# The triangular inverse of a chunked RWKV-7 scan: full 128x128 products against compact 32x32 diagonal blocks

## Chip, cores and metric

One core of a Trainium2 chip runs the whole program. The metric is the device time of one execution in microseconds (us). TensorE multiplies, VectorE and ScalarE work elementwise, GpSimd and SyncE here only issue DMAs. All operands of this part are fp32; the profile shows an fp32 product as two records of weight load and matmul.

## What is computed

Two transformer blocks follow each other on 256 tokens of width 2048; the second has 16 meta tokens in front. Its mixer has an RWKV-7 half and a "fox" attention half. The recurrence of the first, per head of 64 channels (16 heads, 272 tokens), is

```python
def step(S, inp):
    r_t, w_t, k_t, v_t, a_t, b_t = inp
    sa = jnp.einsum('bhvk,bhk->bhv', S, a_t)
    S = (S * w_t[:, :, None, :] + sa[..., None] * b_t[:, :, None, :]
         + v_t[..., None] * k_t[:, :, None, :])
    return S, jnp.einsum('bhvk,bhk->bhv', S, r_t)
_, y = lax.scan(step, jnp.zeros((B, H, N, N), F32), xs)
```

Beside it stand the projections `proj = xn @ w_in`, of which the fox columns (24 tiles of 128) and the gate columns (32 tiles) are computed during the scan.

## The kernel before

**The scan in chunks.** `rwkv_pe`, `rwkv_act` and `rwkv_dve` (L1698, L1973, L2077) hold one stream per engine. A loop over j takes two heads at a time, eight steps in all. The tokens come in a chunk of 16 (meta) and two of 128. Within a chunk the recurrence is solved with the inverse of I - N, N being the strictly upper triangular Gram matrix of b and a, decay included. Index q = 2h + c names head h and chunk c, so a step has four matrices of 128x128 and, for the meta tokens, one of 64x64 that holds two of 16x16 (head h at rows and columns 32h).

**Order of a step on TensorE.** Sums of decays (L1740), the bonus (L1745), transposes to token order (L1752, L1756), the Gram products (L1771, L1773: 64-row halves; L1778: meta, into bank 4), then the inversion, then "x0", "u0", "s0" for the meta chunk (L1843 to L1855), and for each of the chunks "x", "u", "y", state (L1864 to L1891).

**The inversion.** `gm` holds the masked Gram matrices; `upper8` cuts out the 8x8 diagonal blocks, whose inverse comes from the products p2, p4, r (N squared, its square, and the product of the sums). Then blocks are joined to 16, 32, 64, 128: with the inverse R so far and the joining part of N (masks `join16` to `join128`), one product P and one product D per join give the new R. VectorE transposes R between them within 32x32 blocks (`T_`). `product` (L1788) runs over the two matrices of a head, `of_head` (L1783) adds the meta matrix; all products are 128x128x128 up to the join of 64:

```python
for m in (16, 32, 64):
    for h in range(2):
        pe.wait_ge(*rd.after(((f"rt{m // 2}" if m > 16 else "rt", h), j)))
        product(h, 0, 2, 1, m == 16).then_inc(*rp.did(((f"p{m}", h), j)))
        if m > 16 and h == 0:
            side(1)
    for h in range(2):
        pe.wait_ge(*ra.after(((f"p{m}", h), j)))
        last = product(h, 0, 3, 0, m == 16)
```

The last join works on half the columns (L1830, L1837). ScalarE copies the banks to `inv_s` (`step`, L2028 to L2036; L2056 for the last), VectorE masks, adds the identity, transposes (L2137 to L2211). `gram_mask(n, h)` (L2135) masks half of the Gram matrices of a head, 128x512 in one operation: `gram_mask(0, .)` the products of b, which the inversion needs, `gram_mask(1, .)` those of k, which are needed first at L1864.

**Side work.** `side(n)` lets n slots of the projections pass. On TensorE a slot is one call of `side_mm` (L529): six matmuls, 128x128 weights against 272 or 256 columns, lines L538, L540, L542. On ScalarE (`side_hi`, L520) and VectorE (`side_lo`, L525) one operation of 128x512 comes with every second slot; every eighth slot VectorE also takes a finished tile (L1640, L2662). ScalarE's operation waits until TensorE has used the same quarter of the buffer two tiles before. The `side` calls in the three streams are written out by hand; a step has 31 slots on each engine, whichever kernel. They all have to be done; what the scan doesn't take is done behind it.

**Waits.** Each engine counts its own steps in one semaphore (`Order`: `rd` VectorE, `ra` ScalarE, `rp` TensorE), and the order of the steps is written out in `INV_DVE`, `INV_ACT` and `PE_INV`. An engine's stream is executed in order.

## Time and profile before

| | |
|---|---|
| median of 3 executions | 2949.26 us (2948.57 to 2949.82) |
| the profiled execution | 2952.27 us |
| its span, first to last instruction | 2950.2 us |
| mean granted clock of TensorE | 0.997 |
| first Gram product of the first to that of the eighth scan step | 1407.59 to 1775.74 us of the span: 368.15, 52.6 a step |

The page gives for each engine the union of its instructions' times. Rows of a view of lines read: line, engine, operation, out<-in, shapes, count, then busy us, mean ns of one, and idle time ahead with what ended it. Matmuls overlap, so a record is longer than the distance to the next one. PE is TensorE, PEld its weight loads, DVE VectorE, ACT ScalarE.

### The profile page before, as it was taken

Reading aid. Unit: us, or ns where it says so; the run is one execution under the profiler, and the core shown is the slowest. Engines: PE = TensorE matmul, PEld = TensorE weight load, DVE = VectorE, ACT = ScalarE, POOL = GpSimd, SP = SyncE. Lnnn points to the kernel's source line nnn. Section 1 sums busy time; section 2 is a strip of 40 time slices with the busy share of each in tenths; the row PEclk is TensorE's granted clock in tenths of the full one; section 3 lists DMA queues with packets and bytes.
Section 4 is the critical chain, followed back from the end, with each engine's and each line's share of the span. In section 5 each row is a group of like instructions: output and inputs, shape, how many; then the busy total and the mean of one; then the engine's idle time right before and its main releaser. Section 6 shows DMA issues by size and latency. Waiting matters only on the chain.

```text
span 2950.2 us, 51319 instructions
## 1 busy us (share of the span) xinstructions
PE 2917.3 (99%) x21485; PEld 2697.7 (91%) x21485; DVE 1786.5 (61%) x2680; ACT 1251.0 (42%) x1860; POOL 53.2 (2%) x102
## 2 busy tenths in 40 slices
PE   9999999999999999999999999999999999999999
PEld 8999998888889999999898888889998888889999
DVE  5567757566656445755666666666666655665444
ACT  5355444333333344544333443455444333333433
POOL 1000000000000000000000000000000000000000
PEclk9999999999999999999999999999999999999999
DMA  7665445555555555455333335444555555555553
GB/s 240 196 174 166 158 157 174 186 189 182 194 185 185 185 185 186 143 178 149 83 97 87 83 89 139 119 135 156 188 187 180 184 189 187 187 178 197 185 184 132
DMA packets 370314, 484.96 MB, mean 164 GB/s; under 512 B 12359, under 2 KB 181654, under 8 KB 370150
## 3 DMA queue, kind: packets, MB, share of 16 engines
q1 hardware_dynamic: 362752, 471.55, 50.5%
q0 software_dynamic: 4112, 7.88, 0.9%
q10 hardware_dynamic: 3302, 3.39, 0.4%
q8 instruction: 113, 1.85, 0.3%
q14 instruction: 35, 0.29, 0.0%
HBM read 475.76 MB, written 7.01 MB: 164 GB/s over the span
## 4 chain that ended last, share of the span: by engine, by line
PE 91%; DVE 6%; issue 1%; ACT 1%; DMA 0%; DVEq 0%; SPq 0%; ACTq 0%
PE psum L333 19%; PE psum L339 12%; PE psum L338 12%; PE psum L337 12%; PE psum L335 10%; PE psum L538 5%; PE psum L542 5%; PE psum L540 5%; PE psum L1789 3%; DVE w_lo L323 2%; DVE arena L711 1%; PE psum L1771 0%; DVE arena L699 0%; PE psum L2584 0%; DVE act L786 0%
## 5 line engine op out<-in xcount | busy, mean ns | idle before, releaser
L323 DVE TENSOR_TENSOR w_lo<-w_raw,w_hi 128x1024 fp32r<-128x1024 f32 x728 | 858.9, 1221 | 798.2 <-ACT w_hi L314 798.2
L314 ACT ACTIVATE w_hi<-w_raw 128x1024 fp32r<-128x1024 f32 x728 | 731.3, 1052 | 1163.3 <-PE psum L335 592.1
L333 PE MATMUL psum<-act,w_hi 128*128 128x512 f32 x2816 | 990.0, 394 | 8.6 <-issue 4.5
L337 PE MATMUL psum<-act,w_hi 128*128 128x256 f32 (+2 forms) x3024 | 855.3, 283 | 6.7 <-issue 4.5
L339 PE MATMUL psum<-act,w_lo 128*128 128x256 f32 (+2 forms) x3024 | 856.3, 283 | 0.0
L338 PE MATMUL psum<-act,w_hi 128*128 128x256 f32 (+2 forms) x3024 | 856.3, 283 | 0.0
L335 PE MATMUL psum<-act,w_lo 128*128 128x256 f32 x2816 | 790.9, 281 | 0.0
L333 PEld LDWEIGHTS psum<-act,w_hi 128*128 128x128 f32 x2816 | 529.9, 188 | 136.4 <-DVE w_lo L323 11.1
L337 PEld LDWEIGHTS psum<-act,w_hi 128*128 128x128 f32 (+1 forms) x3024 | 572.4, 189 | 10.9 <-issue 8.2
L339 PEld LDWEIGHTS psum<-act,w_lo 128*128 128x128 f32 (+1 forms) x3024 | 572.9, 189 | 0.0
L338 PEld LDWEIGHTS psum<-act,w_hi 128*128 128x128 f32 (+1 forms) x3024 | 569.2, 188 | 0.1
L335 PEld LDWEIGHTS psum<-act,w_lo 128*128 128x128 f32 x2816 | 530.5, 188 | 0.1
L538 PE MATMUL psum<-act,w_hi 128*128 128x256 f32 (+1 forms) x1280 | 390.6, 305 | 0.0
L542 PE MATMUL psum<-act,w_lo 128*128 128x256 f32 (+1 forms) x1280 | 362.4, 283 | 0.0
L540 PE MATMUL psum<-act,w_hi 128*128 128x256 f32 (+1 forms) x1280 | 362.0, 283 | 0.0
L520 ACT ACTIVATE w_hi<-w_raw 128x512 fp32r<-128x512 f32 x320 | 195.6, 628 | 235.4 <-PE psum L542 222.7
L538 PEld LDWEIGHTS psum<-act,w_hi 128*128 128x128 f32 x1280 | 242.1, 189 | 20.4 <-issue 14.6
L525 DVE TENSOR_TENSOR w_lo<-w_raw,w_hi 128x512 fp32r<-128x512 f32 x320 | 211.8, 681 | 78.7 <-ACT w_hi L520 78.3
L540 PEld LDWEIGHTS psum<-act,w_hi 128*128 128x128 f32 x1280 | 242.2, 189 | 1.1
L542 PEld LDWEIGHTS psum<-act,w_lo 128*128 128x128 f32 x1280 | 241.6, 189 | 0.0
L699 DVE TENSOR_REDUCE arena<-psum 128x256 f32<-128x512 f32 x176 | 112.9, 683 | 15.0 <-PE psum L335 14.0
L1789 PE MATMUL psum<-arena 128*128 128x128 f32 (+1 forms) x800 | 113.3, 280 | 2.0 <-DVE arena L2179 0.9
(381 smaller groups left out, 1732.3 us busy)
## 6 DMA issues: line engine op xcount, KB each, us to landing
w_raw<-w_in SPq DMA_DIRECT2D x128, 1024.0 KB, 5.7
w_raw<-w_down SPq DMA_DIRECT2D x88, 1024.0 KB, 5.1
w_raw<-w_gate_up SPq DMA_DIRECT2D x88, 1024.0 KB, 5.0
w_raw<-w_gate SPq DMA_DIRECT2D x44, 1024.0 KB, 5.1
w_raw<-w_up SPq DMA_DIRECT2D x44, 1024.0 KB, 5.1
w_raw<-w_out SPq DMA_DIRECT2D x16, 1024.0 KB, 5.1
w_raw<-w_o SPq DMA_DIRECT2D x16, 1024.0 KB, 5.1
w_raw<-w_branch_a SPq DMA_DIRECT2D x8, 1024.0 KB, 5.1
```

Source lines behind the costliest of these rows:

```text
L314: nc.scalar.activation(w_hi[:, s % 2, 2 * h:2 * h + 2, 0:wd], w_raw[:, s % RAW, 2 * h:2 * h + 2, 0:wd], ACT.Copy).then_inc(hi_ready, 1)
L323: nc.vector.tensor_tensor(w_lo[:, s % 2, 2 * h:2 * h + 2, 0:wd], w_raw[:, s % RAW, 2 * h:2 * h + 2, 0:wd], w_hi[:, s % 2, 2 * h:2 * h + 2, ...
L333: pe.matmul(dst.rearrange("p (h n) -> p h n", h=2), w1, both_parts, start=first, stop=False, skip_group_check=True)
L335: return pe.matmul(dst[:, 0:n], w0, act_hi[:, k, tok], start=False, stop=last, skip_group_check=True)
L337: pe.matmul(dst, w1, act_hi[:, k, tok], start=first, stop=False, skip_group_check=True)
L338: pe.matmul(dst, w1, act_lo[:, k, tok], start=False, stop=False, skip_group_check=True)
L339: return pe.matmul(dst, w0, act_hi[:, k, tok], start=False, stop=last, skip_group_check=True)
L525: nc.vector.tensor_tensor(side_view(w_lo, u % 2, 4 * n, 4), side_view(w_raw, u % RAW, 4 * n, 4), side_view(w_hi, u % 2, 4 * n, 4).bitcast( ...
L538: pe.matmul(dst, hi[:, k], act_hi[:, k, tok], start=k == 0, stop=False, skip_group_check=True)
L540: pe.matmul(dst, hi[:, k], act_lo[:, k, tok], start=False, stop=False, skip_group_check=True)
L542: mm = pe.matmul(dst, lo[:, k], act_hi[:, k, tok], start=False, stop=k == KT - 1, skip_group_check=True)
L1789: return of_head(h, meta, lambda q, m: pe.matmul(ps(bank, q, m), sl(l, q, m), sl(r_, q, m), start=True, stop=True))
```

## The change

The diagonal 32x32 blocks of all matrices are kept compactly: a tile of 128 partitions x 5 x 32 holds, for block b at partitions 32b to 32b + 31 and slot q, the diagonal block b of matrix q; slot 4 holds the meta blocks of the two heads. Up to the join of 32 eight products (p2, r1t, p4, s8, v16, s16, v32, s32) work on these, each block by a 32x32 tile of the array. The factors are the transposed ones, which VectorE makes out of the banks (`turned`). The raw diagonal blocks come from products of their own ("blocks"), ahead of the Gram products. The joins of 64 and 128 are made of products of 32x32 and 64x64 tiles. The table keeps its size (`room`). The diff, cut to its core. Tables and places:

```diff
+    parts["upper8"] = (i < j) & (i // 8 == j // 8)
+    joins = []
+    for m in (16, 32):
+        join = (i // m == j // m) & (i % m < m // 2) & (j % m >= m // 2)
+        joins.append(join * 1.0 - ((i // (m // 2) == j // (m // 2)) & (i < j)))
+    parts["joins"] = np.concatenate(joins, axis=1)
+    parts["ident_blocks"] = i == j
+    parts["room"] = np.zeros((P, 640))
...
+        raw = place(6, BLOCK)
+        (n8, n8t, i8t, p2, p2t, ip2, ip4, r1t, s8) = (place(5, BLOCK) for _ in range(9))
+        nm = place(2, 5, BLOCK)
+        nm16, nm32 = nm[:, 0], nm[:, 1]
+        s8t, v16, s16, s16t, v32, s32t = n8t, p2, p2t, ip2, ip4, n8
+        inv_t, inv64 = place(4, P), place(4, 2 * BLOCK)
+        v64, v128 = place(4, BLOCK), place(4, 2 * BLOCK)
```

TensorE: "blocks" (head 0 from partitions 0 to 63, head 1 from 64 to 127) and the meta products; then the Gram products as before, and the inversion with its waits (`dve(n)` and `act(n)` wait for that step of VectorE or ScalarE):

```diff
+                for b in range(4):
+                    for c in range(2):
+                        t = slice(META + c * P + BLOCK * b, META + c * P + BLOCK * b + BLOCK)
+                        for h, r in enumerate(hs):
+                            pe.matmul(psum[rows32(b), 5 - h, cols32(c)], bh[r, t], ar[r, 0, t],
+                                      start=True, stop=True)
+                for n, src in enumerate((bh, kh)):
+                    for h, r in enumerate(hs):
+                        mm = pe.matmul(psum[mh[h], 5 - h, 64 + n * META:64 + (n + 1) * META], src[r, 0:META],
+                                       ar[r, 0, 0:META], start=True, stop=True)
+                mm.then_inc(*rp.did(("blocks", j)))
...
+                def product(bank, l, r_, step, nq=5):
+                    for q in range(nq):
+                        for b in range(4 if q < 4 else 2):
+                            mm = pe.matmul(psum[rows32(b), bank, cols32(q)], l[rows32(b), q], r_[rows32(b), q],
+                                           start=True, stop=True)
+                    mm.then_inc(*rp.did((step, j)))
...
+                dve("n8t")
+                product(4, n8t, n8, "p2")
+                side(1)
+                dve("ip2")
+                product(5, ip2, i8t, "r1t")
+                act("p2")
+                product(4, p2t, p2, "p4")
+                side(1)
+                dve("ip4")
+                act("r1t")
+                product(4, r1t, ip4, "s8")
+                side(1)
+                dve("s8t")
+                product(5, nm16, s8t, "v16")
+                side(1)
+                act("v16")
+                product(4, v16, s8, "s16")
+                side(1)
+                dve("s16t")
+                product(5, nm32, s16t, "v32", 4)
+                side(1)
+                act("v32")
+                product(4, v32, s16, "s32", 4)
+                side(1)
+                dve("s32t")
+                for q in range(4):
+                    for b in (0, 2):
+                        mm = pe.matmul(psum[rows32(b + 1), 0, cols32(q)], gm[rows32(b), q, cols32(b + 1)],
+                                       s32t[rows32(b), q], start=True, stop=True)
+                mm.then_inc(*rp.did(("v64", j)))
+                side(1)
+                dve("v64")
+                act("s32")
+                for q in range(4):
+                    mm = pe.matmul(psum[rows32(1), 0, cols32(q)], inv_t[rows32(1), q, cols32(1)],
+                                   v64[rows32(1), q], start=True, stop=True)
+                mm.then_inc(*rp.did(("x64t", j)))
+                for q in range(4):
+                    for b in (0, 2):
+                        mm = pe.matmul(psum[rows32(b), 1, cols32(q)], v64[rows32(b + 1), q],
+                                       inv_t[rows32(b + 1), q, cols32(b + 1)], start=True, stop=True)
+                mm.then_inc(*rp.did(("x64", j)))
+                side(1)
+                low, high = slice(0, 64), slice(64, P)
+                dve("x64t")
+                act("x64")
+                for h in heads:
+                    for c in range(2):
+                        q = 2 * h + c
+                        mm = pe.matmul(psum[high, h, 64 * c:64 * c + 64], gm[low, q, high], inv64[low, q],
                                        start=True, stop=True)
+                    mm.then_inc(*rp.did((("v128", h), j)))
+                side(1)
+                for h in heads:
+                    if h:
+                        act("v128")
+                    else:
+                        dve("v128")
+                    for c in range(2):
+                        q = 2 * h + c
+                        mm = pe.matmul(psum[low, 4 + h, 64 * c:64 * c + 64], v128[high, q], inv_t[high, q, high],
                                        start=True, stop=True)
+                    mm.then_inc(*rp.did((("x128", h), j)))
+                side(1)
+                dve("gm0")
...
+                for h in range(2):
+                    mm = pe.matmul(psum[rows32(h), 1, 0:RHD], s16[rows32(h), 4], xs[rows32(h), 0],
+                                   start=True, stop=True)
...
+                    act("x128")
```

ScalarE; v16, s16 (after s16t), v32, s32 (after s32t, four copies by rows), x64 (two), v128 and x128 of head 1 follow with `side(1)` between them:

```diff
-                side(6)
+                side(4)
+                def copy(dst, src):
+                    return s.activation(dst, src, ACT.Copy)
+                def evac(step, of, dst, bank, nq=5):
+                    s.wait_ge(*of)
+                    copy(dst, blocks_of(bank, nq)).then_inc(*ra.did((step, j)))
+                s.wait_ge(*PEA("blocks"))
+                copy(raw[:, 0:2], blocks_of(5, 2))
+                copy(raw[mh[0], 4:6, 0:META], psum[mh[0], 5, 64:64 + 2 * META].rearrange("p (n t) -> p n t", n=2)) \
+                    .then_inc(*ra.did(("raw0", j)))
+                side(1)
+                evac("p2", rd.after(("p2t", j)), p2, 4)
+                side(1)
+                evac("r1t", PEA("r1t"), r1t, 5)
+                side(1)
+                evac("s8", rd.after(("s8t", j)), s8, 4)
```

VectorE:

```diff
-            v.memset(inv_m_all, 0.0)
+            v.memset(raw, 0.0)
+            v.memset(inv_t, 0.0)
+            v.memset(inv64, 0.0)
...
+                v.wait_ge(*PEA("blocks"))
+                v.wait_ge(*rd.after("gm_zero"))
+                v.tensor_copy(raw[:, 2:4], blocks_of(4, 2))
+                v.tensor_copy(raw[mh[1], 4:6, 0:META],
+                              psum[mh[1], 4, 64:64 + 2 * META].rearrange("p (n t) -> p n t", n=2)) \
+                    .then_inc(*D_("raw1"))
+                v.wait_ge(*A_("raw1"))
+                v.wait_ge(*ra.after(("raw0", j)))
+                TT(n8, raw[:, 0:5], table_of("upper8"), ALU.mult).then_inc(*D_("n8"))
+                v.wait_ge(*A_("n8"))
+                v.transpose(n8t, n8).then_inc(*D_("n8t"))
+                v.wait_ge(*A_("n8t"))
+                TT(i8t, n8t, table_of("ident_blocks"), ALU.add).then_inc(*D_("i8t"))
+                v.wait_ge(*PEA("p2"))
+                TT(ip2, blocks_of(4, 5), table_of("ident_blocks"), ALU.add).then_inc(*D_("ip2"))
+                v.transpose(p2t, blocks_of(4, 5)).then_inc(*D_("p2t"))
+                TT(nm, raw[:, 0:5].unsqueeze(1).broadcast_to([P, 2, 5, BLOCK]),
+                   T["joins"].rearrange("p (n t) -> p n t", n=2).unsqueeze(2).broadcast_to([P, 2, 5, BLOCK]),
+                   ALU.mult).then_inc(*D_("nm"))
+                side(1)
+                v.wait_ge(*A_("nm"))
+                TT(nm, nm, T["ident_blocks"].unsqueeze(1).unsqueeze(1).broadcast_to([P, 2, 5, BLOCK]), ALU.add) \
+                    .then_inc(*D_("nm_diag"))
+                v.wait_ge(*PEA("p4"))
+                TT(ip4, blocks_of(4, 5), table_of("ident_blocks"), ALU.add).then_inc(*D_("ip4"))
+                v.wait_ge(*PEA("gram"))
+                gram_mask(0, 0)
+                side(1)
+                gram_mask(0, 1).then_inc(*D_("gram"))
+                def turned(step, of, dst, nq=5):
+                    v.wait_ge(*PEA(of))
+                    v.transpose(dst, blocks_of(4, nq)).then_inc(*D_(step))
+                turned("s8t", "s8", s8t)
+                side(1)
+                gram_mask(1, 0)
+                turned("s16t", "s16", s16t)
                 side(2)
+                turned("s32t", "s32", s32t[:, 0:4], 4)
+                v.wait_ge(*A_("s32t"))
+                for b in range(2):
+                    v.tensor_copy(inv64[rows32(b), :, cols32(b)], s32t[rows32(b), 0:4])
+                for h in range(2):
+                    ins = TT(gm0[mh[h], 0, mh[h]], raw[mh[h], 5, 0:META], mask[mh[h], mh[h]], ALU.mult)
+                ins.then_inc(*D_("gm0"))
```

Behind it come, each after its wait: the copy v64, `side(1)`, x64t, `gram_mask(1, 1)`, `side(1)`, v128 of head 0, `side(1)`, x128 of head 0, `side(2)`.

## Rows read from the trace of the kernel before

**Rows 1.** The page, part 1 and the chain of part 4 by engine.

```profile
PE 2917.3 (99%) x21485; PEld 2697.7 (91%) x21485; DVE 1786.5 (61%) x2680; ACT 1251.0 (42%) x1860; POOL 53.2 (2%) x102
...
PE 91%; DVE 6%; issue 1%; ACT 1%; DMA 0%; DVEq 0%; SPq 0%; ACTq 0%
```

**Rows 2.** Windows p2 to x0, eight steps: us, busy us per engine, clock, DMA.

```profile
1464.10:1488.17 24.07, 23.59 (x182) 21.95 (x183) 17.11 (x49) 10.68 (x30) 0.55 (x1) 1.00 0.21 56
...
1728.25:1751.59 23.34, 23.08 (x182) 21.39 (x183) 17.00 (x49) 10.98 (x31) 0.00 (x0) 1.00 0.17 46
...
sum 190.24, PE 187.30 PEld 174.24 DVE 136.60 ACT 86.97 POOL 4.39; mean PE 23.41 PEld 21.78 DVE 17.07 ACT 10.87 POOL 0.55
```

**Rows 3.** TensorE's timeline, step 2: start us, us, what, count.

```profile
1464.78 0.29 PE L540 MATMUL psum<-act,w_hi 128*128 128x272 f32 x1
...
1466.17 2.37 PE L1789 MATMUL psum<-arena 128*128 128x128 f32 x14
...
1478.97 1.05 PE L1789 MATMUL psum<-arena 128*128 128x128 f32 x8
1479.78 0.37 PE L538 MATMUL psum<-act,w_hi 128*128 128x272 f32 x1
```

**Rows 4.** TensorE's timeline, step 3; the last row is cut at 1515.33.

```profile
1511.22 0.51 PE L1756 MATMUL psum<-tab,arena 64*16 64x64 f32 x12
...
1513.16 0.29 PE L542 MATMUL psum<-act,w_lo 128*128 128x272 f32 x1
1513.38 0.43 PE L1771 MATMUL psum<-arena 64*64 64x256 f32 x2
1513.39 0.43 PE L1773 MATMUL psum<-arena 64*64 64x256 f32 x2
1513.64 0.38 PE L1771 MATMUL psum<-arena 64*64 64x256 f32 x2
...
1513.86 0.38 PE L1771 MATMUL psum<-arena 64*64 64x256 f32 x2
...
1515.26 0.27 PE L1778 MATMUL psum<-arena 64*16 64x16 f32 x8
1515.46 0.39 PE L538 MATMUL psum<-act,w_hi 128*128 128x272 f32 x1
1515.69 0.29 PE L540 MATMUL psum<-act,w_hi 128*128 128x272 f32 x1
...
1517.26 0.71 PE L1789 MATMUL psum<-arena 128*128 128x128 f32 x4
...
1515.26 0.23 PE L1778 MATMUL psum<-arena 64*16 64x16 f32 x5
```

**Rows 5.** Lines by form of step 3: count, busy us, mean ns of one.

```profile
L1756 PE MATMUL psum<-tab,arena 64*16 64x64 f32 x12 | 0.5, 218 | 0.0
...
L1778 PE MATMUL psum<-arena 64*16 64x16 f32 x8 | 0.3, 176 | 0.0
```

**Rows 6.** VectorE's timeline, step 3, as rows 3.

```profile
1515.58 0.69 DVE L2137 TENSOR_TENSOR arena<-psum,tab 128x512 f32<-128x512 f32 x1 [1.29 <-PE psum L1778]
...
1516.76 0.45 DVE L2174 STREAM_TRANSPOSE arena<-arena 128x256 f32<-128x256 f32 x1
```

**Rows 7.** Lines by form of VectorE, then ScalarE, seven steps: as rows 5.

```profile
L525 DVE TENSOR_TENSOR w_lo<-w_raw,w_hi 128x512 fp32r<-128x512 f32 x108 | 72.7, 675 | 7.6 <-ACT w_hi L520 7.6
L2137 DVE TENSOR_TENSOR arena<-psum,tab 128x512 f32<-128x512 f32 x28 | 18.7, 668 | 14.3 <-PE psum L1778 14.3
...
L2191 DVE TENSOR_TENSOR arena<-psum,tab 128x256 f32<-128x256 f32 x14 | 5.3, 416 | 0.2
...
L1640 DVE TENSOR_TENSOR arena<-psum,rstd 128x272 f32<-128x272 f32 x11 | 4.7, 424 | 0.1
...
L2211 DVE COPY arena<-psum 64x128 f32<-64x128 f32 x14 | 4.0, 283 | 12.1 <-PE psum L1837 12.1
...
L2032 ACT ACTIVATE arena<-psum 128x256 f32<-128x256 f32 x126 | 48.3, 383 | 69.6 <-PE psum L1789 68.9
```

More of the change, by code:

```diff
@@ L1589, in transformer_pair_kernel @@
         heads = range(2)
-        INV_DVE = [("gram", 0), ("n8", 0), ("nt8", 0), ("gram", 1), "gram0", ("n8", 1), ("nt8", 1),
-                   ("p2t", 0), ("ip2", 0), ("int8", 0), ("int8", 1), ("p2t", 1), ("ip2", 1),
-                   ("less", 0), ("less", 1), ("nm16", 0), ("nm16", 1), ("ip4", 0), ("ip4", 1)]
-        INV_ACT = ["p2", "r1t", "r"]
-        for m in (16, 32, 64):
-            INV_ACT += [f"p{m}", f"r{m}"]
-            INV_DVE += [(n, h) for n in ["rt" if m == 16 else f"rt{m // 2}", f"nm{2 * m}"][:1 + (m < 64)]
-                        for h in heads]
-        INV_DVE += [(n, h) for n in ("rt64", "r128") for h in heads]
-        INV_ACT = [(n, h) for n in INV_ACT + ["p128"] for h in heads]
+        INV_DVE = ["raw1", "n8", "n8t", "i8t", "ip2", "p2t", "nm", "nm_diag", "ip4", "gram", "s8t", "s16t",
+                   "s32t", "gm0", "v64", "x64t", "v128", "x128"]
+        INV_ACT = ["raw0", "p2", "r1t", "s8", "v16", "s16", "v32", "s32", "x64", "v128", "x128"]
         for j in range(8):
@@ L1614, in transformer_pair_kernel @@
         rw_pe_steps = ["kksum"]
-        PE_INV = ["p2", "p4", "r"]
-        for m in (16, 32, 64, 128):
-            PE_INV += [f"p{m}", f"d{m}"]
-        PE_INV = [(n, h) for n in PE_INV for h in heads]
+        PE_INV = ["p2", "r1t", "p4", "s8", "v16", "s16", "v32", "s32", "v64", "x64t", "x64",
+                  ("v128", 0), ("v128", 1), ("x128", 0), ("x128", 1)]
         rw_pe_steps += [("logits", 0), ("kkspread", 0)]
         for j in range(8):
-            rw_pe_steps += [(n, j) for n in ["sums", "bonus", "toks", "gram"] + PE_INV
+            rw_pe_steps += [(n, j) for n in ["sums", "bonus", "toks", "blocks", "gram"] + PE_INV
                             + ["x0", "u0", "s0", "x1", "u1", "y1s1", "x2", "u2", "y2"]]
@@ L2206, in rwkv_dve @@
[L2206 to L2214 removed]
+                TT = v.tensor_tensor
```

225 lines of the change are left out of this document (53 added, 172 removed).

## The prediction

> **What bounds the kernel now.** I read the page first: TensorE is busy in 99% of a span of 2950.2 us and makes 91% of the chain that ended last; VectorE is at 61%, ScalarE at 42% [rows 1]. So time is saved only where TensorE has less to do, or waits less. Next, the stretches: in each of the eight scan steps the inversion, from its first product to the product "x0", takes 23.34 us (step 7), 24.07 (step 2) and the like, in all eight 190.24, at a granted clock of 1.00 throughout, with TensorE busy for 187.30 of them [rows 2]. Within such a stretch two kinds of work share TensorE: the inversion's own products, and 11 slots of side work (six matmuls of the fox and gate projections each), which must be done somewhere in any case. Side matmuls start 0.126 us apart (11 from 1464.78 to 1466.17), so a slot is 0.76 us and 11 are 8.3 us. What is left, 23.8 - 8.3 = 15.5 us per step, is what the change can touch. A full 128x128 fp32 product is two records, 0.101 us apart (8 in 0.81 us) [rows 3].
>
> **What tiles cost.** The trace shows small tiles at work already. In the Gram products (L1771, L1773) four records of 256 columns on four 64x64 quarters start within 0.02 us of each other, and the next four 0.26 later, then 0.22: four tiles run side by side. L1756 (64 rows x 16 columns, 64 columns moving) alternates between two halves of the rows and writes one bank: 12 records are through in 0.51 us, one lasts 0.218, so starts are (0.51 - 0.22)/11 = 0.027 us apart, half of what a record of 64 columns needs alone (half of the 0.106 of 128 columns). So two run at a time, in one bank. L1778 (16 columns) has 8 records in 0.27 us, one lasting 0.176: 0.013 apart, 0.025 a pair; five have started 0.07 us after the first [rows 4, 5]. Changing between full and tiled work costs: side to tile, 0.22 between starts (1513.16 to 1513.38) for 0.13; tile to side, 0.11 from L1778's last start (0.27 - 0.18 = 0.09 after its first at 1515.26) to the side matmul at 1515.46, and 0.23 instead of 0.13 to the one after it [rows 4]. Together some 0.30 us for each tiled product between two side slots.
>
> The Trainium skill ("TensorEngine Tiling (Array Packing)", Gotcha 1) says that different row tiles cannot access one PSUM bank at the same time. The new products put all four diagonal tiles into one bank, so by that rule they would run one by one; the pairs of L1756 speak against it. That case is a rival below.
>
> **Removed per step:** 50 products in ten rounds, eight half-wide ones, one of u0, i.e. the 15.5 us, waits among them.
>
> **Added per step, on TensorE.** 32 columns are a quarter of 128, so 0.027 us a record; I take 0.03 us for a batch of four tiles (one record each), from the 0.025 of L1778's pairs and four starts at 0.007 each. A product over five blocks is 18 matmuls, 36 records, ten batches: 0.29 us.
> - p2, s8, v16, s16: 4 x (0.30 + 0.29) = 2.36
> - r1t and p4, back to back: 0.30 + 0.58 = 0.88
> - v32, s32 (four blocks): 2 x (0.30 + 0.24) = 1.08
> - v64 (two tiles, 16 records): 0.30 + 0.20 = 0.50
> - x64t (one tile, 8 records) and x64 (two, 16): 0.30 + 0.43 = 0.73
> - v128, x128 (one 64x64 tile each, 8 records of 64 columns at 0.053): 2 x (0.30 + 0.43) = 1.46
>
> Sum 7.0 us. Besides: "blocks", 16 more products ahead of the Gram ones, 32 records in pairs 0.43, one more change of tiling, 0.5; u0 by two tiles 0.2. The small Gram products are moved ahead, not added. The 11 side slots stay 11. The extra clearing on VectorE before the scan is some 570 elements a partition more: 0.6 us at most by the slope of its operations (0.283 for 128, 0.42 for 256 elements [rows 7]), beside side work, taken as nothing; if that cover fails it is 0.6 once.
>
> So without waits 15.5 - 7.0 - 0.5 - 0.2 = 7.8 us a step are saved.
>
> **Waits.** Each product now hands over to VectorE (or VectorE, then ScalarE) and TensorE covers with one side slot, 0.76 + 0.20 of the change back = 0.96 us. From a product's last start to VectorE's start it takes 0.22 us (L1778's last by 1515.36, L2137 at 1515.58), from the end of an operation to the product that waits for it 0.05 (1516.76 + 0.45 to 1517.26) [rows 4, 6]. An operation over 160 elements is 0.32 by the same slope, a copy by ScalarE 0.30 (0.383 for 256 [rows 7]). A hand-over with one operation is 0.22 + 0.32 + 0.05 = 0.6: covered. With a transpose and then ScalarE's copy it is 0.95, just covered, or covered by the next product too (p2t and p2 lie beside r1t). The transposes read the bank directly, so one copy less stands in the chain.
> The hand-over that isn't covered is s8 to v16. VectorE's queue is: ip4, Gram mask, side slot, Gram mask, then s8t. Each mask is 0.668, a side slot on the mean 0.39 (0.675 every second, a take of 0.43 every eighth) [rows 7]. From the start of ip4 that makes 0.32 + 0.67 + 0.39 + 0.67 + 0.32 + 0.05, less 0.25 for overlaps of successive operations: 2.2 us. TensorE in that time waits 0.37 for ip4, does s8 (0.50) and a slot (0.76): 1.6. Behind the wait stand v16 and everything after it. So 0.5 us a step, up to 1.1 where the slot holds both a difference and a take. ip4 itself stands behind nm, a side slot and the diagonal: late by 0 to 0.6. For ip4 and the joins (v64 behind inv64, gm0 and a side slot) I add 0.5: 1.0 in all. VectorE loses some 7 us of work per step (some 27 operations of 0.4 for 18 of 0.2 to 0.45), so it doesn't become the bound as a whole; nor does ScalarE. Blocks come 1.9 us before the Gram products end, so the first operations lie beside these and two slots: p2 doesn't wait.
>
> **The sum.** 7.8 - 1.0 = 6.8 us a step, 8 x 6.8 = 54 us. The profiled execution took 2952.3; 2898 would be left. It stands 3.0 over the median of the runs, 2949.3, so the forecast is 2895 us. After the scan nothing is touched: the same slots have been used.
>
> **Rivals.**
> (A) One tile at a time. 352 records of 32 columns at 0.027 are 9.5 us instead of the 3.3 in my sum: 6.2 more, against which the waits (1.0) are then hidden. 7.8 - 6.2 = 1.6 a step, 12 us: 2937. For it: no row has four 32x32 tiles, or more than 8 small records in a run. Against it: the pairs and fours of [rows 4]. Chance 0.12.
> The skill's page "TensorE: Matmul & The Clock Gate" ("Wait - 56ns, not 53.3ns?") has a floor of about 25 ns between starts however small the product is; by it the time would be about that of this case. L1778's 0.013 us goes below it.
> (B) Slower: supply of instructions. 184 small matmuls are 368 records with as many weight loads. The fastest longer run in the trace is the 40 records from 1513.38 to 1515.46: 0.052 us each [rows 4]; that more can be supplied for 36 in a row isn't shown, since the 8 of L1778 may have been waiting in the queue. At 0.052 they take 19.1 us instead of 4.1, 15 more: 7.2 lost a step, 58 us: 3007. It decides from (4.1 + 7.8)/368 = 0.032 us a record. Against it: those 40 were bound by their own columns, and nothing there waits for supply. Chance 0.07.
> (C) The waits take over: ten hand-overs each 0.3 us beyond the cover, 3 us a step instead of 1.0: 4.8 x 8 = 38, 2911. For it: the old rounds had the other head's product as cover too; VectorE's side operations stand ahead of most transposes. Against it: at most one hand-over works out as uncovered. Chance 0.28.
> The forecast's own case, 2884 to 2902, has 0.53.
>
> **Numbers.** Lower end: all 7.8 us and batches a little faster, 8.2 x 8: 2884. Upper end: (C) whole and (A) in part, 2930; outside stay most of (A) and (B), under 0.2. What a measurement here can tell from no change is 0.2%, 5.9 us. Faster by more: the forecast, (C) and nearly all of (A), 0.91; within: 0.03; slower: 0.06.
>
> **What would show it.** In the stretch from p2 to x0: some 16.3 us a step instead of 23.8, five-block products with 36 records in 0.3 us plus a record's 0.17, starts in fours 0.007 apart; the wait of v16 for s8t as the longest of TensorE in the scan, some 0.5 us. (A) would show starts 0.027 apart, (B) gaps with no releaser ("issue") within a product, (C) waits for VectorE or ScalarE at most products. The forecast is wrong if a five-block product takes over 0.6 us, or if TensorE's waits pass 1.5 us a step.

## The result and the profile after

| | before | changed |
|---|---|---|
| median of four runs, us | 2949.54 (2948.57 to 2949.84) | 2901.72 (2900.59 to 2912.38) |
| profiled execution / its span | 2952.3 / 2950.2 | 2902.6 / 2900.6 |
| records of TensorE | 21485 | 23517 |
| last "yc" product of the scan, from the span's start | 1816.27 | 1762.27 |
| from there to the products of the last gate slice | 39.00 | 42.88 |

The ratio of the changed kernel's time to the time before is 0.9845, 95% interval 0.9834 to 0.9857: faster by 1.6%. The median is 6.7 us above the forecast of 2895 and inside the range. Run once more the changed kernel gave 2899.16.

The page of the changed kernel, its engines, the chain by engine, and the queue that carries instructions, against [rows 1]:

```profile
PE 2862.3 (99%) x23517; PEld 2636.6 (91%) x23517; DVE 1734.1 (60%) x2522; ACT 1223.4 (42%) x1788; POOL 53.0 (2%) x102
...
q8 instruction: 129, 2.11, 0.3%
...
PE 91%; DVE 6%; issue 1%; ACT 1%; DMA 1%; DVEq 0%; SPq 0%; ACTq 0%
```

TensorE does 9% more records in 55 us less of busy time. It is as full as before, so what is read next is where it waits and what a tiled product costs.

The windows from p2 to x0, all eight steps (bounds, us, busy us of each engine, clock, DMA share and GB/s), against [rows 2]:

```profile
1410.84:1427.81 16.97, 16.29 (x404) 13.98 (x404) 10.39 (x26) 7.48 (x20) 0.55 (x1) 1.00 0.26 71
1458.20:1474.00 15.80, 15.80 (x403) 13.80 (x404) 11.21 (x28) 6.78 (x19) 0.54 (x1) 1.00 0.24 65
1503.50:1519.52 16.02, 15.89 (x404) 13.80 (x403) 10.39 (x26) 7.48 (x20) 0.55 (x1) 1.00 0.23 63
...
1595.35:1612.87 17.52, 16.09 (x404) 13.91 (x404) 10.75 (x27) 7.49 (x20) 1.11 (x2) 1.00 0.28 76
...
1733.73:1749.13 15.40, 15.39 (x403) 13.54 (x404) 11.29 (x28) 6.75 (x19) 0.00 (x0) 1.00 0.28 72
sum 129.57, PE 126.73 PEld 110.13 DVE 87.14 ACT 56.85 POOL 3.85; mean PE 15.84 PEld 13.77 DVE 10.89 ACT 7.11 POOL 0.48
```

129.57 us for 190.24: 16.20 a step, forecast 16.3. Steps 1 and 5 stand out, with TensorE idle for 0.7 and 1.4 us inside them.

TensorE's timeline of step 3, from p2 on (start us, us, what, count):

```profile
1503.50 0.52 PE L1792 MATMUL psum<-arena 32*32 32x32 f32 x36
1503.95 0.39 PE L543 MATMUL psum<-act,w_hi 128*128 128x272 f32 x1
...
1504.90 0.84 PE L1792 MATMUL psum<-arena 32*32 32x32 f32 x72
...
1506.63 0.52 PE L1792 MATMUL psum<-arena 32*32 32x32 f32 x36
```

A product is 36 records in 0.52 us, of which the last lasts 0.19: starts 0.33/35 = 0.009 us apart; two in a row (r1t, p4) are 72 records in 0.84. From p2 to r1t there are 1.40 us: 0.33 for the product, 0.76 for the side slot, and 0.31 for the change of tiling and back (taken as 0.30).

TensorE's waits in the scan (engine, line, what it waited for: us in all, times, longest):

```profile
PE psum L1792 <- DVE arena L2190: 4.5, 4, 1.2
PE psum L1792 <- issue: 1.8, 3, 1.3
...
PE psum L1837 <- issue: 0.3, 1, 0.3
PE psum L1738 <- DVE arena L2136: 0.3, 1, 0.3
PE psum L1792 <- DVE arena L2212: 0.2, 1, 0.2
```

L1792 is the product of 32x32 tiles, L2190 the transpose n8t for which p2 waits, L2212 the transposes s8t, s16t and s32t. The wait I had forecast as the longest, v16 for s8t, is the last row. The view lists it once (step 7), but it leaves out idle time of under 0.15 us, and the end of a side matmul covers part of this wait. The starts show more. Step 3, the last matmul of the side slot and v16, then VectorE's s8t:

```profile
1507.80 0.29 PE L547 MATMUL psum<-act,w_lo 128*128 128x272 f32 x1
1508.23 0.52 PE L1792 MATMUL psum<-arena 32*32 32x32 f32 x36
...
1507.83 0.34 DVE L2212 STREAM_TRANSPOSE arena<-psum 128x160 f32<-128x160 f32 x1
```

v16 starts 0.43 us after the side matmul, where the other products of the step start 0.22 after theirs. By the same measure v16 is 0.20 us late in steps 1, 3 and 5, 0.09 in step 6 and 0.29 in step 7: 1.0 us in the scan, for 4 forecast. The longest group of all is one I had put at nothing: p2 waits in four of eight steps. The second group has no releaser, and it lies inside products.

**Where p2 waits.** Step 2, ScalarE, VectorE and TensorE in one timeline (in brackets the idle time before and its releaser):

```profile
1455.02 0.38 PE L1782 MATMUL psum<-arena 64*64 64x256 f32 x2
...
1456.39 0.63 ACT L525 ACTIVATE w_hi<-w_raw 128x512 fp32r<-128x512 f32 x1 [3.23 <-PE psum L547]
...
1457.05 0.29 ACT L2052 ACTIVATE arena<-psum 128x64 f32<-128x64 f32 x2
1457.44 0.33 DVE L2188 TENSOR_TENSOR arena<-arena,tab 128x160 f32<-128x160 f32 x1 [3.42 <-ACT arena L2052]
1457.80 0.35 DVE L2190 STREAM_TRANSPOSE arena<-arena 128x160 f32<-128x160 f32 x1
...
1458.20 0.52 PE L1792 MATMUL psum<-arena 32*32 32x32 f32 x36 [1.09 <-DVE arena L2190]
```

ScalarE's program has four side calls ahead of raw0. In the even steps the last of them is a rounding of weights (L525) that waits 3.23 us for TensorE's side slot, which itself stands behind the Gram products. raw0, ready long before, comes after it, VectorE has been idle for 3.42 us for want of raw0, and TensorE for want of n8t. All three engines wait for an order written by hand.

**Behind the scan.** The last "yc" comes 54.0 us earlier in the span. 0.8 of them lie ahead of the scan, where nothing was meant to change (the first "sums" start at 1399.54 before and 1398.71 now); the scan itself is 53.2 us shorter, for 54 forecast. 3.9 are given back until the products of the last gate slice. TensorE at the sixth gate slice, then four windows (as above) of the stretch behind it:

```profile
1795.04 0.65 PE L1940 MATMUL psum<-small,tab 16*64 16x256 f32 x4 [2.01 <-DMA arena<-rwkv_g]
```

```profile
1790.00:1796.80 6.80, 4.79 (x30) 3.62 (x31) 2.67 (x7) 1.26 (x2) 0.72 (x1) 1.00 0.60 172
1796.80:1803.60 6.80, 6.80 (x28) 5.46 (x27) 3.23 (x7) 0.63 (x1) 0.72 (x1) 0.50 0.06 19
1803.60:1813.80 10.20, 10.20 (x76) 8.11 (x75) 5.05 (x13) 6.12 (x6) 0.00 (x0) 1.00 0.40 104
1813.80:1817.20 3.40, 3.40 (x17) 3.40 (x17) 0.40 (x1) 0.55 (x1) 0.00 (x0) 0.51 0.54 143
```

TensorE waits 2.01 us for a slice of the gate's weights (1.19 before), and then it is granted 0.50, the lower level of 1.2 GHz, for 6.8 us. The kernel before has only the 3.4 us at the end. 0.8 more of waiting, and 3.1 by which the records at the lower clock start later against those before, are the 3.9 given back. The size belongs to this execution: the same kernel run again waits 1.7 us, has 3.4 us at half clock and gives back 2.1.

**The idle time with no releaser.** TensorE in step 5, inside the product s32:

```profile
1604.19 0.37 PE L1792 MATMUL psum<-arena 32*32 32x32 f32 x19
1605.86 0.32 PE L1792 MATMUL psum<-arena 32*32 32x32 f32 x13 [1.29 <-issue]
```

The product's operands are there, since 19 of its 32 records have run. I counted TensorE's instructions (records, weight loads and those of its sequencer, which wait for semaphores and set registers) from the first "sums" of step 1: the four places inside tiled work where two starts lie over 0.4 us apart come at instruction 438, 694, 6581 and 8117, all 181 or 182 over a multiple of 256. The packets of the instruction queue are 16384 bytes each, 256 instructions if one has 64 bytes. The Trainium skill ("Advanced Engine Details and Errata", section ISA Cache) has instructions cached in lines of 16 KB, 256 instructions each, which agrees with the spacing of these gaps. The packet before each gap begins 2.5 to 2.7 us ahead of the gap's end (1603.29 for the one at 1605.86). That is rival (B) in small: the mechanism is there, and it bites now and then.

### The profile page after: what moved, and what is told of

Same layout as the page of the kernel before. It is cut to its first block, busy times and chain, and to the rows that moved or that the text cites. A ratio compares the mean times of both kernels' runs of the same rounds, so it can differ in the third digit from the quotient of the medians.

```text
span 2900.6 us, 55153 instructions
## 1 busy us (share of the span) xinstructions
PE 2862.3 (99%) x23517; PEld 2636.6 (91%) x23517; DVE 1734.1 (60%) x2522; ACT 1223.4 (42%) x1788; POOL 53.0 (2%) x102
## 4 chain that ended last, share of the span: by engine, by line
PE 91%; DVE 6%; issue 1%; ACT 1%; DMA 1%; DVEq 0%; SPq 0%; ACTq 0%
PE psum L338 20%; PE psum L344 12%; PE psum L343 12%; PE psum L342 12%; PE psum L340 10%; PE psum L543 6%; PE psum L547 5%; PE psum L545 5%; DVE w_lo L328 2%; PE psum L1792 1%; DVE arena L716 1%; PE psum L1780 0%; DVE arena L704 0%; PE psum L2611 0%; DVE act L791 0%
## 5 line engine op out<-in xcount | busy, mean ns | idle before, releaser
L547 PE MATMUL psum<-act,w_lo 128*128 128x256 f32 (+1 forms) x1280 | 363.6, 284 | 0.0
L525 ACT ACTIVATE w_hi<-w_raw 128x512 fp32r<-128x512 f32 x320 | 195.6, 628 | 235.0 <-PE psum L547 222.0
L2052 ACT ACTIVATE arena<-psum 32x128 f32<-32x128 f32 (+5 forms) x128 | 33.8, 270 | 63.4 <-DVE arena L2212 24.5
```

What stands on the lines that cost most here:

```text
L525: nc.scalar.activation(side_view(w_hi, u % 2, 4 * n, 4), side_view(w_raw, u % RAW, 4 * n, 4), ACT.Copy).then_inc(hi_ready if n % 2 else si ...
L547: mm = pe.matmul(dst, lo[:, k], act_hi[:, k, tok], start=False, stop=k == KT - 1, skip_group_check=True)
```

## The experiments

All on the changed kernel. "Scan" is from the first "sums" to the last "yc" of the profiled execution, "gap" the distance of two starts in s32 of step 5. The ratio is to the kernel before, run beside it.

| kernel | median us | ratio, 95% interval | scan | gap | half clock in the scan, us |
|---|---|---|---|---|---|
| changed | 2901.72 | 0.9845 [0.9834, 0.9857] | 363.6 | 1.5 | 0 |
| changed, again | 2899.16 | 0.9836 [0.9820, 0.9852] | 363.9 | 2.0 | 0 |
| same tile in a row | 2966.97 | 1.0039 [1.0013, 1.0065] | 429.9 | none | 99 |
| products twice | 2965.21 | 1.0046 [1.0031, 1.0060] | 432.7 | many | 51 |
| copy, then transpose | 2903.26 | 0.9833 [0.9816, 0.9849] | 369.0 | 1.6 | 13.7 |
| masks late | 2898.75 | 0.9817 [0.9801, 0.9833] | 367.8 | 1.5 | 13.7 |
| raw0 early | 2900.99 | 0.9832 [0.9818, 0.9845] | 363.7 | 1.9 | 10.2 |
| third gate slice | 2897.59 | 0.9825 [0.9811, 0.9838] | 363.8 | 1.9 | 0 |
| the last two | 2895.50 | 0.9817 [0.9803, 0.9830] | 359.8 | 2.2 | 0 |
| the last two, masks late | 2890.12 | 0.9795 [0.9781, 0.9808] | 363.7 | 1.7 | 13.7 |
| these three, slot | 2890.88 | 0.9798 [0.9784, 0.9811] | 358.2 | 0.9 | 0 |
| these three, 256 instructions on | 2892.03 | 0.9801 [0.9787, 0.9814] | 363.4 | 1.5 | 13.7 |
| these three, 128 instructions on | 2888.15 | 0.9789 [0.9776, 0.9803] | 355.1 | none | 0 |

The medians belong to other executions than the profiled one, and whether the clock falls differs from one execution to the next (the three with masks late had 2895.76 in the profiled execution and 2888.7 to 2890.6 in the four others). So a cause is read from the scan column and the waits, and a version is judged by its median.

**1. The changed kernel again.**

> The changed kernel once more, for the pairing with the three beside it. Theory 1 (the time missing against the forecast lies in ScalarE's second side operation before raw0, 1.2 us in every second step, and in the wait for the gate slices behind the scan with the slower clock after it): 2900.6 to 2902.6 us, the same 1.2 us waits at p2 in steps 2, 4, 6 and 8 and about 2 us at the gate slices. Rival (these waits are chance of one execution): waits at other places or of other lengths, at an equal total.

2899.16, a little under the range of theory 1; in its trace p2 waits 4.5 us in four steps again, the gate slice 1.7, and s32 of step 5 has its gap, 1.99 us. The places are properties of the program, not of a run; the lengths of the gaps and of the half clock differ between the two.

**2. Same tile in a row** (rival A's case).

```diff
-                    for q in range(nq):
-                        for b in range(4 if q < 4 else 2):
+                    for b in range(4):
+                        for q in range(nq if b < 2 else 4):
```

> Only the order of the 32x32 products inside each five-block product is changed: all matrices of one diagonal tile in a row, then the next tile, instead of the four tiles in turn. The work and the waits are the same. Theory A (four tiles run side by side only when their products alternate): each record of 32 columns then stands behind the one before on its own tile, 0.027 us each, 36 records 0.95 us instead of 0.33, eight products in eight steps: up to 40 us more, less what the waits of every second step hide; 2930 to 2942. Theory B (the queue in front of the array looks far enough ahead to take products of other tiles first): nearly unchanged, within 5 us. Theory C (tiles do not run side by side at all and the records are merely short): unchanged, 0.33 us.

The same products in the other order, each tile's five blocks one after another. TensorE's timeline of step 1, then two windows:

```profile
1410.49 1.02 PE L1792 MATMUL psum<-arena 32*32 32x32 f32 x36
...
1412.39 1.76 PE L1792 MATMUL psum<-arena 32*32 32x32 f32 x72
```

```profile
1427.80:1461.80 34.00, 32.91 (x361) 28.81 (x362) 18.12 (x49) 10.66 (x26) 3.19 (x6) 1.00 0.48 131
1461.90:1496.00 34.10, 34.10 (x383) 30.42 (x381) 12.80 (x31) 7.74 (x20) 1.09 (x2) 0.50 0.15 40
```

36 records now take 1.02 us: starts (1.02 - 0.19)/35 = 0.024 us apart, where four alternating tiles have 0.009. So tiles run side by side only if neighbours in the queue are of different tiles, and the 0.027 of rival (A) was the right price for its case. A second loss I had in no case: after a stretch in which TensorE was busy for 32.9 of 34.0 us the clock is granted at 0.50 for 34.1 us. It did not wait there for anything longer than p2's 1.1 us. Each of the three such stretches begins 1.2 to 2.7 us after that wait of p2, which in the changed kernel has no half clock behind it. The whole gain is gone, by these two. The ten executions lie between 2935.12, at a mean granted clock of 0.993, and 2973.66, at 0.978; so the order alone costs about what theory A had (2930 to 2942), and the rest goes with the clock.

**3. Products twice** (rival B, forced: 36 records become 72 and so on, nothing else).

```diff
-                    for q in range(nq):
+                    for q in [*range(nq), *range(nq)]:
```

> Every five-block (and four-block) product is made twice, the same values written twice to the same bank, no side slot between. It measures what one such product costs at the margin. Theory A (bound by the tiles, no lack of instructions): 0.33 us more for each of six and 0.26 for two, 2.5 us a step, 20 us: 2921. Rival (supply of instructions: 72 records and as many weight loads in a row are more than the queue can hold ahead): the second half runs slower, 0.5 us or more each, 30 to 60 us.

TensorE's timeline of step 2, then its waits in the scan:

```profile
1466.62 1.49 PE L1792 MATMUL psum<-arena 32*32 32x32 f32 x144
...
1469.00 0.24 PE L1792 MATMUL psum<-arena 32*32 32x32 f32 x2
1470.47 0.79 PE L1792 MATMUL psum<-arena 32*32 32x32 f32 x70 [1.23 <-issue]
```

```profile
PE psum L1792 <- issue: 23.2, 23, 2.0
...
PE psum L543 <- issue: 4.0, 1, 4.0
```

Where instructions are at hand, 144 records run at 0.009 us each, as fast as 36. But in the dense stretches the next block of 256 is late nearly every time: 27.2 us of idle time, every gap at 181 or 182 modulo 256. In a row of late blocks (the gaps ending at 1470.47, 1473.93, 1478.03, 1481.77) they come 3.46 to 4.10 us apart, 3.77 on the mean: 0.0147 us an instruction, 0.029 a record with its weight load. The changed kernel asks for 84 instructions every 1.40 us (72 of the product, 12 of a slot), 0.0167 each: it just gets by. 8 x 2.5 us of second products, 25.1 more of gaps (27.2 for 2.1) and 21 to 26 for the 51 us at the lower clock (0.42 of them by experiment 5, or half) are 66 to 71, measured 68.8 more in the scan.

**4. Copy, then transpose** (the transposes of s8 and s16 no longer read the bank).

```diff
-                turned("s8t", "s8", s8t)
+                v.wait_ge(*ra.after(("s8", j)))
+                v.transpose(s8t, s8).then_inc(*D_("s8t"))
...
-                evac("s8", rd.after(("s8t", j)), s8, 4)
+                evac("s8", PEA("s8"), s8, 4)
```

> Undoes one part: s8 and s16 are copied out of the bank by ScalarE first, and VectorE transposes the copy, as the kernel before did. The chain from product to transpose is longer by ScalarE's copy and one hand-over, 0.35 us. Theory (a side slot and the change of tiling cover 0.96 to 1.07 us; s8t has 0.2 us of wait already in every second step, s16t none): s16t 0.95 us, covered; s8t behind the Gram masks anyway: under 2 us more in all. Rival (the direct transposes are a main part of the gain): 2 x 0.35 x 8 = 5.6 us more.

The ratios, 0.9833 and 0.9836, are the same, and v16 starts as late behind s8t as before, step for step within 0.01 us. The scan is 5.1 us longer, but has 13.7 us at half clock, behind the gap of step 5, and such a stretch costs 5.7 (experiment 5). Not told apart from no effect: the direct reading isn't what made the change fast.

**5. Masks late** (both Gram masks behind s8t; `gram_mask(1, 0)` also moves, from ahead of s16t to behind it).

```diff
-                v.wait_ge(*PEA("gram"))
-                gram_mask(0, 0)
-                side(1)
-                gram_mask(0, 1).then_inc(*D_("gram"))
+                side(1)
...
                 turned("s8t", "s8", s8t)
+                v.wait_ge(*PEA("gram"))
+                gram_mask(0, 0)
+                gram_mask(0, 1).then_inc(*D_("gram"))
```

> VectorE masks the Gram matrices of b behind s8t instead of ahead of it, the hand-over that I had forecast as uncovered (0.5 us a step). What the profile of the changed kernel shows of it is 0.20 to 0.27 us in every second step: theory 1 expects 0.5 to 1 us less, which is within the noise, and no wait of v16 in the trace. Rival (the masks now push s16t or v64 back): more, with waits at v32 or x64t.

The wait of v16 for s8t is gone, from the list of waits and from the starts: v16 starts 0.20 to 0.22 us behind the side matmul in every step, 1.0 us less in all than in the changed kernel. That is theory 1's size. The ratio is 0.0019 lower, within the intervals. So the queue that I had costed at 4 us (0.5 a step) was worth 1.0. This trace also gives the price of the half clock: over the 13.7 us at 0.50 the records fall back by 5.7 us against the same records of the changed kernel.

**6. raw0 early.** ScalarE makes two side calls ahead of raw0 and three behind, for four and one.

```diff
-                side(4)
+                side(2)
...
                     .then_inc(*ra.did(("raw0", j)))
-                side(1)
+                side(3)
```

> ScalarE lets two side slots pass before it copies the raw blocks and three behind, instead of four and one. Theory 1: the wait of p2 for n8t (1.2 us in four of eight steps) goes, 4.7 us less, about 2896; p2 starts 2.0 us after the last Gram product in every step. Rival 1 (VectorE's queue, not ScalarE, holds n8t back): no change. Rival 2 (the side operations moved behind raw0 now stand before the copy of p2, and r1t or p4 waits instead): under 2 us less, with new waits at p4 or s8.

TensorE's waits in the scan and behind it:

```profile
PE psum L1792 <- issue: 2.5, 4, 1.7
PE psum L1940 <- DMA arena<-rwkv_g: 1.6, 1, 1.6
...
PE psum L1792 <- DVE arena L2212: 0.2, 1, 0.2
```

The 4.5 us of p2 are gone, by the cause that was named, and the scan is no shorter: 363.7. The median of 2900.99 misses the 2896 of theory 1. The next window shows where they went; it begins 2 us behind the gap of step 5.

```profile
1605.80:1616.00 10.20, 10.20 (x71) 9.15 (x69) 4.70 (x12) 2.12 (x6) 0.54 (x1) 0.50 0.18 45
```

By the starts of the same records in both traces, these 10.2 us at half clock cost 4.3, and the gap of step 5 is 0.4 longer: together what p2 no longer waits.

**7. Third gate slice.** A third buffer, in a tile that is free by then, so that three slices are under way.

```diff
-                b, c = j % 2, slice(j * P, (j + 1) * P)
-                if j >= 2:
-                    g.wait_ge(*rp.after(("out", j - 2)))
+                b, c = j % 3, slice(j * P, (j + 1) * P)
+                if j >= 3:
+                    g.wait_ge(*rp.after(("out", j - 3)))
```

> Three buffers for the gate slices behind the scan instead of two (the third in a tile that is free then). Theory 1: the wait of 2.0 us for the sixth slice goes, and with it the stretch of 6.8 us at half clock that followed it in the changed kernel (0.5 to 2.9 us more): 2 to 5 us less, 2896 to 2899. Rival (the slower clock stretch there comes from the small products around it, not from the idle time): 2 us less and the half clock stays.

The wait for the slice is gone, so is the half clock behind it, and the stretch to the products of the last gate slice is 37.67 us, 5.2 less than in the changed kernel and 1.3 less than before. It is 37.67 in the traces of all six kernels with the third buffer, and 39.35 to 44.89 in those of the seven others. What was given back behind the scan is explained. The medians alone would not show it: 2897.59 and, for the changed kernel run beside it, 2899.16, with intervals that overlap. A wait for the slice also doesn't always bring the half clock: in experiment 6 it was 1.6 us, and none followed.

**8. Both.**

> Both edits. They lie in different stretches, so theory 1 expects their sum: 7 to 9.5 us less than the changed kernel, 2891 to 2894. If one hides the other: less than the sum.

2895.50, above the 2891 to 2894 expected. With no half clock in the scan this time the waits of p2 show at last: 359.8 for 363.8 with the third slice alone, 4.0 of 4.5 us.

**9. All three.**

> The changed kernel with three edits at once: the ScalarE side calls moved out from ahead of raw0, the third gate-slice buffer, and the two Gram masks behind s8t. Theory: what is left over of the changed kernel's waits are p2 in the even steps (4 x 1.2 us), the gate slice (2 us and its half-clock stretch) and single gaps of supply; the first two edits together gave 2895.5. The third edit frees the hand-over s8 to v16, which waits only 0.2 us in odd steps, so it should give at most 1 us more: 2893 to 2896. Rival (the masks held TensorE by more than the trace shows, since the side slot behind s8 hides part of it): 2889 to 2892. Rival (the late masks make v64 or x0 wait): 2898 or more.

2890.12, at a ratio of 0.9795 for 0.9817. That is in the rival's range, but the intervals overlap, so the 5 us in favour of the late masks are not shown. The starts give them 1.0 us, as in experiment 5, and part of the rest is the clock: the execution that is the median of "both" was granted 0.996, the one here 0.998. At 0.997 each, "both" took 2892.5 and 2894.4 us and this kernel 2888.7 and 2890.6. The waits that are left in the scan:

```profile
PE psum L1794 <- issue: 2.5, 4, 1.5
PE psum L1752 <- DVE arena L2159: 0.3, 1, 0.3
PE psum L1740 <- DVE arena L2138: 0.3, 1, 0.3
```

All but 0.6 us of what TensorE waits for in the scan is now supply, and the clock falls to half for 13.7 us right behind it.

**10 to 12: is it the place or the count?** The first adds a side product between v16 and s16, one fewer behind y1s1.

> All three edits, and one more side product between v16 and s16 in each step (two in place of one), one fewer behind y1s1. Theory (supply): the dense stretch of a step then asks for its instructions over 0.76 us more, and the gaps inside products of steps 5 and 6 shrink by about 0.76 us each or go; with them the half-clock stretch behind: 1 to 4 us faster than the same kernel without the slot. Rival (the supply gap depends on where fetches fall, not on the mean density): gaps of the same size in the same steps, and no difference, within 1 us. Rival (the slot behind y1s1 hid a wait for ys or state_h): each step 0.3 to 0.7 us longer, 2 to 5 us slower.

The gap of step 5 shrinks from 1.67 to 0.91, by 0.76, one slot; no half clock in the profiled execution, scan 5.6 us shorter. In step 6 the theory failed: a gap of 0.8 us stands there, where the kernel without the slot has none. In the medians, nothing (2890.88), since most executions of the kernel without the slot had kept their clock.

The second and third put unread products ahead of the first "sums":

```diff
+                for n in range(64 if j == 0 else 0):
+                    pe.matmul(psum[rows32(n % 4), 5, 480:512], ident[rows32(n % 4), 0:BLOCK],
+                              ident[rows32(n % 4), 0:BLOCK], start=True, stop=True)
```

> All three edits, and 64 small 32x32 products (128 instructions with their weight loads, some 0.5 to 0.9 us) ahead of the first sums of step 1, whose results nobody reads. They move every later instruction by half of 256 places. Theory (instructions come to TensorE in blocks of 256, and a gap opens where a block comes late): gaps inside products lie at counts of 54 (not 182) modulo 256 from the first sums of the unshifted numbering, that is, still at the same absolute places modulo 256 of the whole stream, and so at other products than before; the gap inside s32 of step 5 (1.3 to 2.2 us) is gone or sits in another product and step. Rival (the gap belongs to that place of the program, for example to a DMA or an engine active then): it stays inside s32 of step 5, 1.3 to 2.2 us. Time: that of the unshifted kernel plus 0.5 to 0.9 us, less up to 2 us where no block comes late, plus up to 5 us if a late one pulls the clock to half.

It moved nothing, and that was my mistake: each such product is two records with a weight load each, so 64 of them are 256 instructions, a whole block. The gap stayed in s32 of step 5, 1.55 us. With half as many:

> The three edits, and 32 unread 32x32 products ahead of the first sums of step 1: 64 records and 64 weight loads, since the identity operand makes two records of each, so 128 instructions (the kernel with 64 such products moved everything by exactly 256 and so changed nothing). Theory (instructions come in blocks of 256): counted from the first sums, gaps inside products move from 182 to 54 modulo 256; none lies inside s32 of step 5, nor inside the second product of step 1 where the kernel without the shift has +0.6 us; others may open in other products. Rival (the gap belongs to that place of the program): s32 of step 5 keeps its gap of 1.3 to 2.2 us, at count 181. Time: 2890.1 plus 0.5, less 1.5 to 6 if no block comes late in the dense stretch (gap and half-clock stretch behind it), plus up to 5 if two do.

TensorE in s32 of step 5, first with the three edits alone, then with 128 instructions more:

```profile
1599.44 0.37 PE L1794 MATMUL psum<-arena 32*32 32x32 f32 x19
1601.29 0.32 PE L1794 MATMUL psum<-arena 32*32 32x32 f32 x13 [1.48 <-issue]
```

```profile
1601.07 0.45 PE L1797 MATMUL psum<-arena 32*32 32x32 f32 x32
1601.45 0.39 PE L543 MATMUL psum<-act,w_hi 128*128 128x272 f32 x1
```

The gap is gone. The one gap left inside a product, +0.48 us in step 4, lies at 54 modulo 256, where it was forecast. Idle time without a releaser falls from 2.5 to 0.3 us:

```profile
PE psum L1797 <- issue: 0.3, 1, 0.3
```

There is no half clock in the scan, which takes 355.1 us, 8.6 less than without the 64 useless records: 2.2 of idle time, and the rest goes with the 13.7 us at half clock. The median, 2888.15, is lower by 2, which the intervals don't tell apart, since the kernel without them had kept its clock in most executions; its own five lie within 2 us (2887.52 to 2889.48), those without within 7. It is the fastest of all, 2.1% under the kernel before and 11 us under the changed kernel run again (ratios 0.9789 and 0.9836, whose intervals do not overlap).

**Why step 5.** In the ten kernels without the 128 instructions, with alternating tiles and products made once, the gap of step 5 is the largest, 0.9 to 2.2 us; in the 3.5 us ahead of it the 16 DMA engines are 0.69 to 1.0 busy, with the side work's 1 MB load of weights. Two windows, the changed kernel ahead of its gap, and the shifted one ahead of the same boundary, in that order:

```profile
1599.90:1603.20 3.30, 3.17 (x117) 2.75 (x116) 1.62 (x4) 1.54 (x4) 0.00 (x0) 1.00 0.92 245
```

```profile
1592.30:1595.70 3.40, 3.40 (x145) 2.94 (x147) 2.63 (x7) 1.33 (x4) 0.56 (x1) 1.00 0.02 6
```

In the first the load was issued at 1599.19 and the instruction packet begins at 1603.29, 6.7 us after the one before it; in the second the packet begins at 1595.79, just as its load starts. The gaps of these kernels with a DMA share of 0.02 to 0.03 ahead are 0.36 to 0.62 us. In experiment 3, where the blocks are asked for without a pause, gaps of 1.4 to 1.7 us have the same low share ahead (those that end at 1470.47 and 1749.04), so a load isn't needed for a gap of this size. That the packet stands behind the load's packets is the reading that fits; no run moved the load alone, so for step 5 this is argued and not shown. Shown are the spacing of 256 and that the gaps move with the count.

## Why the prediction was right, and where not

- **The sum.** Forecast 54 us by the end of the scan, measured 53.2 in the scan, with misses that cancel, which is luck. Waits: 8.0 forecast, 7.6 measured (4.5 of p2, 2.1 of supply, 1.0 of v16), so the size was right and the places were not: of the 4.0 forecast at v16 a quarter was there, and p2 and supply had been put at nothing. Products: 7.0 a step forecast, 7.5 measured (15.80 of a window without waits, less 8.3 of slots), 3.8 us too few in all. Blocks: 1.8 too many. 54.4 + 0.4 - 3.8 + 1.8 = 52.8; the 0.4 that are left I can't place. Neither sign of being wrong was seen: a five-block product takes 0.52 us, and TensorE's waits are under 1.5 us a step.
- **The tiled product.** 0.29 forecast, 0.33 measured; changes of tiling 0.30 and 0.31. v32 and s32 0.24 and 0.26; v64 0.20 and 0.25; x64t with x64 0.43 and 0.40; v128 and x128 0.43 and 0.46. The argument from L1756 and L1778, that 32x32 tiles would run side by side in one bank, held. The Trainium skill ("TensorEngine Tiling (Array Packing)", Gotcha 1) has different row tiles barred from one PSUM bank at the same time; four of them at 0.009 us between starts in one bank speak against that. The floor of about 25 ns from start to start that the Trainium skill gives ("TensorE: Matmul & The Clock Gate", "Wait — 56ns, not 53.3ns?") is met only in experiment 2 (24 ns), where one tile is used over and over; alternating tiles go below it.
- **Blocks** were taken at 0.43 us as pairs. They are 64x32 tiles, and 32 records ran in 0.20. Mis-sized by 0.23 a step, about 2 us in all.
- **s8 to v16**, "the hand-over that isn't covered", 0.5 us a step. VectorE's side of it was right (2.2 forecast; ip4 at 1505.79, s8t done at 1508.17, 2.4). TensorE's side was wrong: I let it wait 0.37 us for ip4, but ip4 was done at 1506.12, half a us before the side slot in front of s8 ended (1506.63). Those 0.5 us were the missing cover. The wait was 0.2 to 0.3 us in the odd steps and at most 0.1 in the even ones, and experiment 5 removes it.
- **"p2 doesn't wait"** failed. I costed the hand-over blocks to n8 to n8t to p2 as work beside the Gram products, and did not look at what ScalarE has queued ahead of raw0. Experiment 6 shows it.
- **"After the scan nothing is touched"** failed: it is true of the work, not of when its data come. The same two buffers and the same loads come to a TensorE whose surroundings have moved, and the wait grew by 0.8 us and was followed by 6.8 us of half clock. Experiment 7 shows that both go with the third buffer. By the profiled executions, 2898 forecast and 2902.6 measured, the 3.9 us are most of 4.6; in the kernel run again they are 2.1, so of the 6.7 us between the medians they are a part whose size isn't known.
- **Rival (B)** had 0.07 as a bound on all records. Its deciding price, 0.032 us a record in runs of 36, was the wrong quantity: runs of 36 are never bound (0.009), the mean over 256 instructions is, at about 0.0147 each (experiment 3).
- **Rival (C)** was right for two hand-overs: p2 in four steps and, for 0.1 to 0.3 us, v16 in five. **(A)** is excluded by the rows of the changed kernel (0.009 us from start to start); experiment 2 shows that its price, 0.027 us a record, is about that of one tile (0.024).

## What to carry to other kernels

Small tiles are worth their changes of tiling (0.31 us a pair here) if neighbouring instructions go to different tiles; the loop over tiles belongs inside. Once a stretch is dense in short instructions, count instructions per us as a resource like any other, and spread the long ones between them. Before a wait is costed at nothing, read the queue of every engine on its path up to the operation, side work above all; and a shorter stretch moves all loads behind it.

## What the hardware showed

- Four 32x32 tiles of one bank start 0.009 us apart in long runs (144 records in 1.49 us); one tile over and over 0.024.
- Idle time inside products lies at places that are multiples of 256 of TensorE's instructions apart, and moves with the count (experiments 11 and 12). Where block after block is late, one comes 3.5 to 4.1 us after the last (experiment 3).
- The granted clock fell to half after single gaps of 1.5 to 1.9 us in dense tiled work (for 10 to 14 us), in some executions and not in others: gaps of 1.5, 1.9, 2.0 and 2.2 us had no half clock behind them. In experiment 2 it fell, for 31 to 34 us, 1.2 to 2.7 us after waits of 1.1 us. Which of the gaps brings it isn't settled.
- 13.7 us at half clock cost this stretch of small products and side slots 5.7 us (experiment 5), 10.2 us cost 4.3 (experiment 6).
